# Where a norm's factor and scaled tile live, and which engine adds the squares, in the turnovers of a two-block transformer kernel

## The reference, cut to what matters

```python
x = x + gt * (y @ w_last)                     # last product of the layer, gated sum
f = rsqrt(mean(x * x, axis=-1) + 1e-6)        # one factor per token
h = x * f * g * (1 + sc) + sh                 # scaled, then shifted
z = h @ w_next                                # first products of the next layer
```

## Time and profile before

| what | value |
|---|---|
| median of three runs | 2850.42 us |
| lowest and highest run | 2848.86, 2854.05 us |
| the profiled execution's own time | 2847.69 us |
| its span in the profile | 2845.7 us |
| mean granted TensorE clock | 0.978 |
| busy share of the span: TensorE, VectorE, ScalarE, GpSimd | 92%, 55%, 39%, 39% |

### The profile page before, as it was taken

One profiled execution on the slowest core, in us unless ns is written; L12 is line 12 of the kernel. 1 busy time (PEld: TensorE's weight loads), 2 busy tenths in 40 slices (PEclk: granted clock), 3 DMA queues, 4 the chain that ended last, 5 costly groups with the idle time before them and its releaser, 6 DMA issues. The chain is left out here.

```text
span 2845.7 us, 39462 instructions
## 1 busy us (share of the span) xinstructions
PE 2625.9 (92%) x15228; PEld 2195.1 (77%) x15228; DVE 1556.1 (55%) x2396; ACT 1101.0 (39%) x2033; POOL 1100.2 (39%) x611
## 2 busy tenths in 40 slices
PE   3898989899999899998899999998999997899998
PEld 2665668788888767776788888888888886788887
DVE  5345337754555445656666555546668666722224
ACT  2353442332332455555422112125655545422222
POOL 3336525544544321212333232334444443344444
PEclk9998999999999999999999999999999998999999
DMA  6544214433333100001133333321111110132222
GB/s 235 198 154 163 77 58 152 144 121 135 131 134 125 45 23 23 27 26 46 69 138 133 111 112 133 114 87 57 41 47 56 55 51 31 38 109 97 98 96 75
DMA packets 81609, 267.83 MB, mean 94 GB/s; under 512 B 8720, under 2 KB 16528, under 8 KB 81424
## 3 DMA queue, kind: packets, MB, share of 16 engines
q1 hardware_dynamic: 78000, 257.59, 26.1%
q10 hardware_dynamic: 3136, 6.42, 0.6%
q0 software_dynamic: 288, 1.31, 0.1%
HBM read 260.57 MB, written 4.72 MB: 93 GB/s over the span
## 5 line engine op out<-in xcount | busy, mean ns | idle before, releaser
L2185 POOL TENSOR_TENSOR SLO<-RAW,SHI 128x1024 fp32r<-128x1024 f32 (+1 forms) x335 | 822.3, 2458 | 1242.4 <-ACT SHI L2016 1236.9
L2016 ACT ACTIVATE SHI<-RAW 128x1024 fp32r<-128x1024 f32 (+1 forms) x335 | 345.3, 1035 | 1034.7 <-PE PS L2450 1031.4
L2448 PE MATMUL PS<-HLh,SHI 128*128 128x512 f32 (+1 forms) x1800 | 705.4, 392 | 17.4 <-DVE HLl L2254 8.7
L2449 PE MATMUL PS<-HLl,SHI 128*128 128x512 f32 (+1 forms) x1800 | 680.8, 378 | 0.0
L2450 PE MATMUL PS<-HLh,SLO 128*128 128x512 f32 (+1 forms) x1800 | 680.7, 378 | 0.0
L2448 PEld LDWEIGHTS PS<-HLh,SHI 128*128 128x128 f32 x1800 | 342.8, 190 | 90.4 <-issue 28.5
L2450 PEld LDWEIGHTS PS<-HLh,SLO 128*128 128x128 f32 x1800 | 342.2, 190 | 64.0
L2449 PEld LDWEIGHTS PS<-HLl,SHI 128*128 128x128 f32 x1800 | 343.2, 191 | 59.7 <-issue 5.3
L2448 PE MATMUL PS<-hh,SHI 128*128 128x512 f32 (+1 forms) x1016 | 365.8, 360 | 13.3 <-DVE XL L2326 8.0
L2450 PE MATMUL PS<-hh,SLO 128*128 128x512 f32 (+1 forms) x1016 | 356.5, 351 | 0.0
L2449 PE MATMUL PS<-hl,SHI 128*128 128x512 f32 (+1 forms) x1016 | 354.8, 349 | 0.0
(11 more groups left out here) (255 smaller groups left out, 3931.4 us busy)
## 6 DMA issues: line engine op xcount, KB each, us to landing
RAW<-in_k_w SPq DMA_DIRECT2D x317, 512.0 KB, 3.5
ADA<-in_k_w SPq DMA_DIRECT2D x132, 512.0 KB, 4.3
early<-in_k_w SPq DMA_DIRECT2D x12, 512.0 KB, 18.1
RAW<-in_k_w SPq DMA_DIRECT2D x18, 256.0 KB, 2.6
XL<-in_xT ACTq DMA_DIRECT2D x4, 512.0 KB, 13.6
bi<-in_k_bias SPq DMA_DIRECT2D x16, 128.0 KB, 3.5
out<-XL SPq DMA_DIRECT2D x16, 128.0 KB, 1.8
bi<-in_k_bias SPq DMA_DIRECT2D x8, 192.0 KB, 4.4
```

What stands on the lines that cost most here:

```text
L2016: eng.activation(u.hi, u.w, ACT.Copy).then_inc(S["a_hi"], 1)
L2185: eng.tensor_tensor(u.lo, u.w, u.hi.bitcast(F32), ALU.subtract).then_inc(S["g_lo"], 1)
L2448: eng.matmul(st.out, lh, rh, start=st.first and j == 0, stop=False)
L2449: eng.matmul(st.out, lh, rl, start=False, stop=False)
```

## The change

- The addition of square 7 goes from VectorE to GpSimd, everywhere; the step on VectorE is deleted.
- In the last part of a turnover three squares (tiles 5, 6 and 7) stay apart instead of two. Three cells are taken from the ring of scaled tiles for them, so five are left of eight in T1, T2, T3 and T6, nine of twelve in T4 and T5.
- In turnovers with keys, banks are held from before the first sum to the end of the stage. Each of the last parts gets one for its factor, as far as banks remain beside those of the keys: both parts in T1, T2 and T5, the two latent parts in T3, all three in T4. The logarithm and the exponential write there, and NormA reads the factor from PSUM.
- Where more than one bank is still left (three in T1 and in T5), these become the ring of scaled tiles: NormA writes them, the high and low part read them.
- So the sums rotate over three banks in T1 and T5, six in T2 and T3, five in T4, and eight in T6. Held banks are given back with the last step of every engine as their condition.

```diff
-        if sq.late and k >= 6:
+        if sq.late and k >= sq.split:
...
-        on = "v" if k == 7 else "g"
-        t_add = tick(on + "_sqadd")
-        put(Square(x, s.ap[:, 0:sq.T], a, sq.T, t_x, s.free, [t_sq] + sq.tok, False, on, t_add))
+        t_add = tick("g_sqadd")
+        put(Square(x, s.ap[:, 0:sq.T], a, sq.T, t_x, s.free, [t_sq] + sq.tok, False, "g", t_add))
...
-        b = take()
+        b = take() if sq.bank is None else sq.bank
...
+        out = a if sq.bank is None else b.ap
+        put(Rstd(out, [(a, sq.tok)] + [(s.ap[:, 0:sq.T], t) for s, t in sq.apart], b.ap[:, 0:sq.T], b.free, t_mm, t_ln, t_rs))
...
+        if sq.bank is not None:
+            return b, t_rs
...
+        W = {"f": scaled or W["f"]}
...
-        st.late = [st.f.cells.pop(), st.f.cells.pop()]
+        st.late, st.split = [st.f.cells.pop() for _ in range(3)], 5
+        held, scaled = [], None
+        if keys:
+            room = 8 - sum(1 + ctx for _, _, ctx in keys)
+            for _, _, st in accs[max(0, len(accs) - room):]:
+                held.append(take())
+                st.bank = Cell(held[-1].ap[:, 0:st.T], held[-1].free)
+            if room - len(held) > 1:
+                spare = [take() for _ in range(room - len(held))]
+                scaled = Ring([])
+                scaled.cells = [Cell(b.ap[:, 0:256], b.free) for b in spare]
+                held += spare
...
+        for b in held:
+            give(b, all_now())
```

More of the change, by code:

```diff
@@ L152, in __init__ @@
         self.T, self.cell, self.f, self.tok, self.late, self.apart = T, W["r"].next(), W["f"], [], [], []
+        self.split, self.bank = 6, None
 class Part:
@@ L557, in rstd @@
         a = sq.cell.ap[:, 0:sq.T]
-        b = take()
+        b = take() if sq.bank is None else sq.bank
         work[0] += 4 * sq.T
         t_mm, t_ln, t_rs = tick("p_stat"), tick("a_ln"), tick("a_rs")
-        put(Rstd(a, [(a, sq.tok)] + [(s.ap[:, 0:sq.T], t) for s, t in sq.apart], b.ap[:, 0:sq.T], b.free, t_mm, t_ln, t_rs))
+        out = a if sq.bank is None else b.ap
+        put(Rstd(out, [(a, sq.tok)] + [(s.ap[:, 0:sq.T], t) for s, t in sq.apart], b.ap[:, 0:sq.T], b.free, t_mm, t_ln, t_rs))
         for s, _ in sq.apart:
             s.free = [t_mm]
+        if sq.bank is not None:
+            return b, t_rs
         give(b, t_ln)
@@ L884, in sums, with normed_part @@
                 h.free = [t]
-    def normed_part(part, st, cf, t_cf, shift, W, hfree):
+    def normed_part(part, st, cf, t_cf, shift, W, hfree, scaled=None):
+        W = {"f": scaled or W["f"]}
         rs = rstd(st)
@@ L916, in turnover @@
                 now += 1
-            side.append(norm_of(part, st))
+            side.append(norm_of(part, st, scaled))
             starts.append(now + wait)
@@ L1421, in build_program @@
              [(p, gates(0, 2), Stats(256, H2)) for p in lats], [],
-             lambda p, st: normed_part(p, st, cf, t_cf, lambda k: (mod(0, 3, k), mtok(0, 24 + k)), H2, obu),
+             lambda p, st, f: normed_part(p, st, cf, t_cf, lambda k: (mod(0, 3, k), mtok(0, 24 + k)), H2, obu, f),
              ffn_first(0, False), 5)
@@ L1459, in build_program @@
     turnover(*ffn_end(hid, 0), [(p, gates(0, 5), Stats(256, H2)) for p in lats], [ctx],
-             lambda p, st: normed_part(p, st, cf, t_cf, lambda k: (mod(1, 0, k, 0), mtok(1, k)), H2, hfree),
+             lambda p, st, f: normed_part(p, st, cf, t_cf, lambda k: (mod(1, 0, k, 0), mtok(1, k)), H2, hfree, f),
              [("qkv", c, True) for c in (*kcols, qcols(0))], 5)
@@ L1578, in with_ctx @@
         turnover(*us, [(p, gates(layer, part, int(p is ctx)), Stats(256, H2)) for p in (ctx, *lats)], [],
-                 lambda p, st: normed_part(p, st, *(cfc if p is ctx else cfl),
-                                           lambda k: (mod(at, norm_part, k, int(p is ctx)), mtok(at, 8 * norm_part + k)),
-                                           H2, hfree), keys, wait)
+                 lambda p, st, f: normed_part(p, st, *(cfc if p is ctx else cfl),
+                                              lambda k: (mod(at, norm_part, k, int(p is ctx)), mtok(at, 8 * norm_part + k)),
+                                              H2, hfree, f), keys, wait)
         joined(lats, ctx)
@@ L1949, in build_program @@
              [(p, gates(2, 2, 0), Stats(256, H2)) for p in lats], [],
-             lambda p, st: normed_part(p, st, cf, t_cf, lambda k: (mod(2, 3, k, 0), mtok(2, 24 + k)), H2, hfree),
+             lambda p, st, f: normed_part(p, st, cf, t_cf, lambda k: (mod(2, 3, k, 0), mtok(2, 24 + k)), H2, hfree, f),
              ffn_first(2, False), 5)
@@ L1960, in build_program, with final_part @@
     outv = out.rearrange("(k p) n -> k p n", p=128)
-    def final_part(part, st):
+    def final_part(part, st, _):
         r, t_r = rstd(st)
@@ L2240, in setup @@
                     eng.tensor_scalar(o, col(c), 0.125, None, ALU.mult).then_inc(S["v_g8"], 1)
[L2242 to L2245, removed]
             def norm_a(st):
@@ L2422, in final @@
                                          op1=ALU.mult).then_inc(S["v_out"], 1)
-            own = {Setup: setup, Square: square_, NormA: norm_a, NormB: norm_b, Ada: ada_, Coef: coef_, VCopy: vcopy, HNorm: hnorm, HRope: hrope, Score: score, Flip: flip_,
+            own = {Setup: setup, NormA: norm_a, NormB: norm_b, Ada: ada_, Coef: coef_, VCopy: vcopy, HNorm: hnorm, HRope: hrope, Score: score, Flip: flip_,
                    Share: share, OutNorm: onorm, GMul: gmul, GSum: gsum, Resid: resid, Up: up, HMask: hmask, Zero: zero, LowerB: lowerb,
```

## The result

| | kernel before | kernel after |
|---|---|---|
| median | 2852.03 us of 4 runs (2848.86 to 2854.05) | 2830.5 us of 4 runs (2825.56 to 2832.2) |
| the profiled execution's own time | 2847.69 us | 2830.11 us |
| its span | 2845.7 us | 2828.2 us |
| TensorE busy, mean granted clock | 92%, 0.978 | 93%, 0.98 |

The forecast was 2832.4 us in a range of 2822 to 2843. By the medians the change is 21.5 us, by the two profiled executions 17.5 us of span: the profiled execution of the kernel before is 4.3 us faster than its median, that of the kernel after lies at its median. So about 4 us of the gain are in no comparison of the two profiles.

What follows compares the result with a forecast made beforehand. TensorE, busy 92%, was taken as the bound, so time is won only in its waits or lower clock. Terms -5 - 3.8 - 1 - 2.5 - 1 - 4 - 1.5 + 0.8 = -18.0 took 2850.4 to 2832.4 us, range 2822 to 2843.

Steps and rivals of the forecast that it cites:

- Start, -5: Program start: modulation products no longer stand behind addition 7 on VectorE; first low part between 38.5 and 43.5, -5 us.
- T1, -3.8: First turnover, three banks: PSUM NormA and NormB escape GpSimd; eighth low part's matmuls end at 567.5, not 571.3: -3.8 us.
- T5, -4: Fifth turnover, as the first with sums of three matmuls: eighth tile ends earlier than 2475.6, -4 us (-5.5 to -2).
- T3, -2.5: Third turnover: VectorE's two blocks go, GpSimd's additions set the pace; first key near 1367, -2.5 us (-4 to 0).
- T2 and T4, -1 each: Second and fourth turnover: keys wait for a weight's rest, so GpSimd's queue; -1 us each (-2 to 0, -2.5 to +1).
- T6, -1.5: Sixth turnover: GpSimd has four additions, begun earlier, instead of five before the last factor; -1.5 us (-2 to -1).
- The fourth term, +0.8: Last part's ones matmul: a fourth term is two matmuls more, 0.25 us, on the path in three stages or so: +0.8.
- A NormA in PSUM: NormA with factor and output in PSUM, not in the trace: priced at the gated sum's 0.40 us, at most 0.95.
- The sum: Whole program: all terms together give -18.0 us, so the median goes from 2850.4 to 2832.4 us.

Runs made afterwards that it cites:

- two late squares: Changed kernel with two squares instead of three kept apart in a stage's last part (tile 5's square added on GpSimd again): 2827.23 us, ratio 0.9911.
- three edits: Changed kernel plus start's factor and scaled tiles in PSUM with two squares apart, T1/T5 spare banks taken at first NormA, two squares apart instead of three: 2824.9 us.
- these with T5 as changed: Kernel of the three edits, but in the fifth turnover the spare banks are taken ahead of the sums, as in the changed kernel: 2822.19 us, ratio 0.9899.

## Why the prediction was right

- **Start, -5**: -5.9, by the mechanism named. Products and additions took turns (a product near 2 us), the first low part ended at 41.16 (near 42 was forecast), and putting the addition back costs the same 6.0. What reached T1 was 4.3.
- **T1, -3.8**: -3.9. In the time of before (4.3 us added) the factor's matmul came at 556.5 (557.9 forecast), the first key at 560.2 (561.2), the eighth tile's end at 567.3 (567.5). The low clock lay over the first sums for 6.8 us, as taken, not over the keys. Two things were missed: TensorE also stands 3.88 us before its first sum, which costs about 2 us against six banks, and T1 before had a second low stretch, 3.4 us at 554.2, besides the 6.3 us that rows 8 give for the stretch at 561.0.
- **T5, -4**: -4.2. In the time of before the factor's matmul came at 2460.1 (2460.3), the key at 2463.5 (2463.8).
- **T3, -2.5**: -3.4. The logarithm came at 1362.6 in the time of before, as forecast; the context's NormA took 1.01 and 1.04, a little over the 0.95 that was taken. The first key came at 1367.8, 0.8 later than the 1367 forecast. The rest, 1.2 us, was won behind it, where TensorE's next wait for a low part is 1.07 us instead of 1.95; the forecast had nothing there. So up to the first key the term was over-sized, and as a whole under-sized by 0.9.

```profile
1354.85 0.46 ACT L2041 ACTIVATE r<-PS,SMALL 128x256 f32<-128x256 f32 x1
...
1356.30 1.01 DVE L2261 SCALAR_TENSOR_TENSOR f<-XC,COEF,r 128x256 f32<-128x256 f32 x1 [3.49 <-POOL r L2207]
...
1360.06 0.55 PE L2460 MATMUL PS<-HCh,SHI 128*128 128x256 f32 x1 [6.36 <-DVE HCl L2266]
```

- **T2 and T4, -1 each**: -1.8 and -2.3. Both terms counted only GpSimd's queue and left out that VectorE's gated sums no longer stand behind its addition; undoing that move costs T4 5.0 us (beside held banks) and T2 1.0. T4's keys wait for a gated sum, as foreseen for five banks, 3.14 us instead of 3.74 for the rest.

```profile
1922.12 0.55 PE L2460 MATMUL PS<-HCh,SHI 128*128 128x256 f32 x1 [3.14 <-DVE XL L2338]
```

- **T6, -1.5**: -0.8. The factor came sooner, but SP's sixteen issues end the program.
- **The fourth term, +0.8**: two late squares are 0.9 faster in T1 and 0.9 in T3, and three save nothing in T6. The size fits, though a mark hardly settles it.
- **A NormA in PSUM**: 0.48, against 0.47 in SBUF with GpSimd idle. The forecast's 0.40 is the distance from one to the next. The Trainium skill (VectorE: DVE Perf Modes, section The TRN2 errata) gives 120 cycles for a source in PSUM where it gives 58 for one in SBUF, which is 65 ns more at 0.96 GHz as an estimate. That does not show: 0.01 us here, 0.01 at 512 columns (0.76 against 0.75).
- **The rule behind all this**: NormA with one tensor in SBUF takes 0.48 beside a rest, with two 2.19 and 2.58. The Trainium skill (SBUF — State Buffer, section Who interferes with whom) says that a VectorE instruction with at most one SBUF input (outside the 2-port modes) does not contend with GpSimd, and that one with two contends with a GpSimd instruction that reads SBUF; the rows agree in both.
- **The sum** came out within 2 us of the median and 0.5 of the span (-17.5 against -18.0) partly by luck. By the spans, 3.5 us too little for the stages stand against 4.7 us given back between them. By the medians the change was larger than forecast: -21.5 us, and the forecast's own ratio, 2832.4 / 2850.42 = 0.9937, lies just outside the measured interval (0.9908 to 0.9934). The time fitted because the forecast started from the median of three runs, 2850.42, while all later medians of the kernel before are 2851.67 to 2854.11. Where these 4 us lie is open. They are between executions of the kernel before: its mean granted clock is 0.978 in one of 2847.53 us and 0.974 in one of 2855.51 us, and only a fast one has a profile. What is given back was not fully settled either. For 966 to 1344 the profile shows a low stretch of 3.4 us at 1041.3 that the profile before does not have, and four kernels without that stretch (no scaled tile in PSUM, addition back in the turnovers, three edits, and these with T5 as changed) kept 1.6 us more there. For the rest, that the low stretches fall differently is seen in the profiles, and that nothing else differs was only argued.

## What to carry to other kernels

Before a step is left on an engine because the engine has time, look at what stands behind it in its queue: VectorE was 55% busy, and one addition on it, put back, cost 9 us in the turnovers (0.4 us each) and 5 at the start (0.7 us). Where VectorE and GpSimd work side by side, one operand in a free PSUM bank spares an instruction the wait: here 0.48 us instead of 2.19 to 2.58, and banks that nothing uses yet (the scores' at the start) are the first to take. A bank has its price too: taken before the sums, three of them made TensorE stand 2 us longer in T1. And before two kernels are compared stage by stage, take a second profile of one of them: it tells which differences are smaller than chance.

## What the runs showed of the hardware that was not expected

- Kernels that differ in one stage differ by 1 to 3 us in stretches where no step differs, and there the granted clock's low stretches (16 to 21 of 3.4 to 13.7 us in each profile) fall differently. In one profile a delay of 6.0 us at the start was 3.2 at the end; whether a delay decays in general is not shown.
- In a stretch of identical steps the clock was granted at half or in full, here the kernel after and, at about the same time, the one before:

```profile
1041.30:1044.70 3.40, 3.40 (x29) 3.07 (x30) 1.35 (x2) 0.63 (x2) 1.43 (x1) 0.50 0.25 77
```

```profile
1041.30:1060.00 18.70, 16.00 (x122) 11.71 (x122) 9.77 (x20) 10.26 (x24) 5.79 (x5) 1.00 0.09 29
```

- Sixteen output transfers of 128 KB were issued by SP at 0.50 us each, which is longer than the 0.40 us in which VectorE makes one's data.
- Two executions of one program had the same span to 0.1 us with marks up to 1.7 us apart on the way.
